# Attention in a hybrid decoder step: two heads' scores as row tiles, weighted sums as alternating column tiles, the sample's weighted sum in four column tiles

## The reference, cut to what matters

```python
s = jnp.einsum('bnqrhd,bnkrhd->bnrhqk', qb, kc) + bias      # scores, ALiBi bias
p = jnp.exp(s - lse[..., None])                             # three window patterns
o = jnp.einsum('bnrhqk,bnkrhd->bnqrhd', p, vc)              # weighted sum of the values
...
kg = k_ext[:, idx]; vg = v_ext[:, idx]                      # sample rows: gathered cache rows
s = jnp.einsum('bshd,bsjhd->bshj', q, kg) - slopes * offs
o = jnp.einsum('bshj,bsjhd->bshd', p, vg)
...
o_att = jnp.sum(mix_w[..., None] * o_stack, axis=0).reshape(B, T, D_ATT) * jax.nn.silu(g_a)
```

## Time and profile before

| | |
|---|---|
| median of the runs | 1742.71 us |
| span of the profiled execution | 1741.7 us (the runs' time lies 1.0 us above it; the page gives the execution no time of its own beside the span) |
| PE busy | 1626.1 us, 93% |
| DVE, ACT, POOL busy | 814.8, 571.7, 529.7 us |
| projection matmuls, L442, three forms | 595.6, 531.6, 531.5 us |
| phase B, 8 pairs | seven pairs of 72.00 us from one `ssum` to the next, then 75.07 us |

### The profile page before, as it was taken

The page is one execution under the profiler, slowest core; times in us unless marked ns, Lnnn a source line. Parts: engine busy times, 40 slices in busy tenths (PEclk is TensorE's granted clock), DMA queues, the critical chain, the costliest instruction groups (busy, mean ns, idle before and its releaser), DMA issues.

```text
span 1741.7 us, 32851 instructions
## 1 busy us (share of the span) xinstructions
PE 1626.1 (93%) x12525; PEld 1491.2 (86%) x12525; DVE 814.8 (47%) x1326; ACT 571.7 (33%) x935; POOL 529.7 (30%) x256
## 2 busy tenths in 40 slices
PE   5999989999899998999989999999999999789998
PEld 4988979889798897988979988898888988569998
DVE  3145564655646557465575544263443634420000
ACT  5242232422324223232242333334343343432221
POOL 0333232232322323223142223232232332433432
PEclk9999999999999999999999999999999999899999
DMA  5320220302203022030220544435344363525443
GB/s 185 93 73 18 63 58 3 105 13 62 58 1 103 17 63 58 1 96 25 56 73 26 131 104 121 88 99 139 78 121 98 89 139 78 153 73 146 127 113 87
DMA packets 249819, 140.88 MB, mean 81 GB/s; under 512 B 11053, under 2 KB 242798, under 8 KB 249198
## 3 DMA queue, kind: packets, MB, share of 16 engines
q1 hardware_dynamic: 228156, 126.23, 28.2%
q10 hardware_dynamic: 21570, 13.23, 2.5%
HBM read 124.11 MB, written 15.26 MB: 80 GB/s over the span
## 4 chain that ended last, share of the span: by engine, by line
PE 84%; DVE 7%; issue 4%; ACT 1%; DMA 1%; SPq 1%; POOL 1%; DVEq 0%; ACTq 0%; POOLq 0%
PE acc L442 50%; PE head_banks L858 5%; PE head_banks L882 5%; PE head_banks L1035 2%; PE head_banks L1062 2%; PE head_banks L1017 2%; PE head_banks L894 2%; DVE AREN L1523 2%; PE head_banks L1029 1%; DVE AREN L1585 1%; PE head_banks L792 1%; PE head_banks L759 1%; DVE AREN L1763 1%; PE head_banks L775 1%; PE head_banks L910 1%
## 5 line engine op out<-in xcount | busy, mean ns | idle before, releaser
L426 POOL TENSOR_TENSOR WL<-WR,WH 128x1024 fp32r<-128x1024 f32 (+1 forms) x164 | 397.8, 2426 | 943.4 <-ACT WH L418 935.2
L442 PE MATMUL acc<-XH,WH 128*128 128x260 f32 (+1 forms) x2624 | 595.6, 308 | 20.1 <-POOL XL L692 10.3
L442 PE MATMUL acc<-XL,WH 128*128 128x260 f32 (+1 forms) x2624 | 531.6, 284 | 0.0
L442 PE MATMUL acc<-XH,WL 128*128 128x260 f32 (+1 forms) x2624 | 531.5, 284 | 0.0
L442 PEld LDWEIGHTS acc<-XH,WH 128*128 128x128 f32 (+1 forms) x2624 | 412.0, 191 | 59.6 <-issue 29.3
L442 PEld LDWEIGHTS acc<-XL,WH 128*128 128x128 f32 (+1 forms) x2624 | 408.2, 190 | 0.0
L442 PEld LDWEIGHTS acc<-XH,WL 128*128 128x128 f32 (+1 forms) x2624 | 407.5, 190 | 0.0
L418 ACT ACTIVATE WH<-WR 128x1024 fp32r<-128x1024 f32 (+1 forms) x164 | 171.7, 1047 | 147.0 <-PE acc L442 123.9
L652 POOL TENSOR_TENSOR AREN<-AREN,CA 128x1024 f32<-128x1024 f32 x40 | 87.0, 2176 | 163.6 <-PE head_banks L858 81.3
L1226 ACT ACTIVATE AREN<-head_banks 128x512 f32<-128x512 f32 x80 | 47.9, 599 | 215.2 <-PE head_banks L894 114.1
L858 PE MATMUL head_banks<-AREN 128*128 128x128 f32 x640 | 89.4, 299 | 22.0 <-DVE AREN L1585 19.3
(11 more groups left out here) (234 smaller groups left out, 1939.1 us busy)
## 6 DMA issues: line engine op xcount, KB each, us to landing
WR<-in_w_in SPq DMA_DIRECT2D x128, 512.0 KB, 4.1
WR<-in_w_out SPq DMA_DIRECT2D x32, 512.0 KB, 5.8
out<-AREN ACTq DMA_DIRECT2D x32, 256.0 KB, 2.7
AREN<-in_cache_k_win SPq DMA_DIRECT2D x16, 384.0 KB, 8.5
AREN<-in_cache_v_win SPq DMA_DIRECT2D x16, 384.0 KB, 8.6
mix_scratch<-AREN ACTq DMA_DIRECT2D x16, 260.0 KB, 2.6
AREN<-in_x_prompt SPq DMA_DIRECT2D x4, 1024.0 KB, 7.9
AREN<-in_cache_k_win SPq DMA_DIRECT2D x8, 512.0 KB, 7.3
```

The costliest lines, as they stand in the source:

```text
L426: pool.tensor_tensor(WL[:, k % 2, :, 0:M], WR[:, k % 4, :, 0:M], WH[:, k % 2, :, 0:M].bitcast(F32), ALU.subtract).then_inc(s_lo, 1)
L442: mm = pe.matmul(acc[0:M, hf, 0:HT], w[:, k % 2, j, 0:M], x[:, kt, hf * HT:(hf + 1) * HT], start=(kt == 0 and n == 0), stop=(kt == KT - 1 ...
```

## The change

- The order of the steps becomes block by block: (b, h) = (0,0), (0,1), (1,0), (1,1) and so on.
- `QP` with its zero halves becomes `QN`. The scores of the two heads are two matmuls with 64 rows each, on partitions 0 to 63 and 64 to 127, into banks 0 and 1, issued one behind the other. They wait for the largest value (`mx`) of the second head of the block before.
- The weighted sums of both heads are issued together after the second head's transposes, alternating between output partitions 0 to 63 and 64 to 127. They are written to the same 128 columns of bank 3 for every block, so DVE multiplies by the gate block by block (`mixed`, step mo{b}), and the second head's transposes go to bank 3 also and wait for mo{b-1}.
- `av` has twelve matmuls of 256 columns instead of six of 512: the weights have 32 columns (16 used, 16 zero), and the four groups of output columns go to partitions 0, 32, 64 and 96 of one bank. ACT copies once, and `avt` is two transposes of 128 by 128. DVE's last product is four operations instead of two.
- `BEHIND_B` has 12 units at `qb` instead of 14, none at the first head's score, 2 at the second's, 2 at every transpose; the rest moves behind `avt`. `BEHIND_LAST` is as before.
- The copy `QS` of the sample queries falls away; one DVE operation forms `QN` instead of two.

```diff
-JS = [(h, b) for h in range(2) for b in range(QB)]
-BEHIND_B = {"ssum": 6, "tokv": 2, "stok": 2, "qb": 14,
-            **{f"s{j}": (1, 1, 2, 2)[j % QB] for j in range(len(JS))},
-            **{f"t{j}": (1, 2, 2, 2)[j % QB] for j in range(len(JS))},
+JS = [(h, b) for b in range(QB) for h in range(2)]
+BEHIND_B = {"ssum": 6, "tokv": 2, "stok": 2, "qb": 12,
+            **{f"s{j}": 2 if j % 2 else 0 for j in range(len(JS))},
+            **{f"t{j}": 2 for j in range(len(JS))},
             "sct": 4, "pwt": 3, "av": 2}
+PT_BANK = (2, 3, 2, 3, 2, 3, 2, 1)
...
-                    pe.matmul(HB[:, j % 2, 0:n], QP[:, h, 128 * b:128 * (b + 1)], KN[:, 0:n], start=True, stop=True)\
-                        .then_inc(b_pe, PE_B.one(f"s{j}"))
-                    fill(f"s{j}")
+                    pe.wait_ge(b_dve, DVE_B.at(i, f"mx{2 * b - 1}" if b else "pr2"))
+                    for h in range(2):
+                        rows = slice(HD * h, HD * (h + 1))
+                        pe.matmul(HB[:, h, 0:n], QN[rows, 128 * b:128 * (b + 1)], KN[rows, 0:n], start=True, stop=True)\
+                            .then_inc(b_pe, PE_B.one(f"s{2 * b + h}"))
+                    fill(f"s{2 * b + 1}")
...
+                for b in range(QB):
+                    if b + 1 < QB:
+                        score(b + 1)
+                    for h in range(2):
+                        j = 2 * b + h
+                        pe.wait_ge(b_dve, DVE_B.at(i, f"pn{j}"))
+                        pe.wait_ge(b_act, ACT_B.at(i, f"tp{j - 1}" if j else "stok"))
+                        if h and b:
+                            pe.wait_ge(b_dve, DVE_B.at(i, f"mo{b - 1}"))
+                        for t in range(b + 1):
+                            mm = pe.transpose(HB[:, PT_BANK[j], 128 * t:128 * (t + 1)], PP[:, h, 128 * t:128 * (t + 1)], ident)
+                        mm.then_inc(b_pe, PE_B.one(f"t{j}"))
+                        fill(f"t{j}")
+                    pe.wait_ge(b_act, ACT_B.at(i, f"tp{2 * b + 1}"))
                     for t in range(b + 1):
+                        for h in range(2):
+                            cols = slice(HD * h, HD * (h + 1))
+                            mm = pe.matmul(HB[cols, 3, 384:512], VTOK[:, t, cols], PTR[:, h, 128 * t:128 * (t + 1)],
+                                           start=(t == 0), stop=(t == b), skip_group_check=True)
...
-                for q in range(2):
-                    for t, n in enumerate(TS):
-                        mm = pe.matmul(HB[0:16, 2 * q, :], PW[0:n, t, :],
-                                       VC[0:n, t, 4 * q:4 * q + 4, :].rearrange("p b c -> p (b c)"),
-                                       start=(t == 0), stop=(t == 2))
+                for t, n in enumerate(TS):
+                    for q in range(4):
+                        mm = pe.matmul(HB[32 * q:32 * (q + 1), 2, 0:256], PW[0:n, t, :],
+                                       VC[0:n, t, 2 * q:2 * q + 2, :].rearrange("p b c -> p (b c)"),
+                                       start=(t == 0), stop=(t == 2), skip_group_check=True)
...
-                for b in range(NB):
-                    mm = pe.transpose(HB[:, 1, 16 * b:16 * (b + 1)], PRF[0:16, 128 * b:128 * (b + 1)], ident[0:16, 0:16])
+                for e in range(2):
+                    mm = pe.transpose(HB[:, 1, 128 * e:128 * (e + 1)], OS[:, e, :], ident)
...
+                def mixed(b):
+                    dve.wait_ge(b_pe, PE_B.at(i, f"o{b}"))
+                    if b == 0:
+                        dve.wait_ge(o_mix, done(PAIRS, i, 16))
+                    q = slice(128 * b, 128 * (b + 1))
+                    dve.tensor_tensor(MIXB[:, q], HB[:, 3, 384:512], GGB[:, q], ALU.mult).then_inc(b_dve, DVE_B.one(f"mo{b}"))
...
                     if j + 2 < nj:
                         largest(j + 2)
+                    if j and h == 0:
+                        mixed(b - 1)
```

More of the change, by code:

```diff
@@ L1361, in pair_b @@
                     feed(f"s{j}")
+                for j in range(2):
                     exps(j)
@@ L1364, in pair_b @@
                     n = 128 * (b + 1)
-                    if j + 2 < nj:
+                    if h == 0 and j + 2 < nj:
                         feed(f"s{j + 2}")
+                        feed(f"s{j + 3}")
                     act.wait_ge(b_pe, PE_B.at(i, f"t{j}"))
-                    act.activation(PTR[:, j % 2, 0:n], HB[:, 2, 0:n], ACT.Copy).then_inc(b_act, ACT_B.one(f"tp{j}"))
+                    act.activation(PTR[:, j % 2, 0:n], HB[:, PT_BANK[j], 0:n], ACT.Copy).then_inc(b_act, ACT_B.one(f"tp{j}"))
                     if j + 2 < nj:
@@ L1391, in pair_b @@
                 act.wait_ge(b_pe, PE_B.at(i, "av"))
-                for q in range(2):
-                    avc = act.activation(PRF[0:16, 512 * q:512 * (q + 1)], HB[0:16, 2 * q, :], ACT.Copy)
-                avc.then_inc(b_act, ACT_B.one("avc"))
+                act.activation(OS.rearrange("p e c -> p (e c)"), HB[:, 2, 0:256], ACT.Copy).then_inc(b_act, ACT_B.one("avc"))
                 feed("av")
@@ L1703, in pair_b @@
                                          op0=ALU.mult, op1=ALU.mult).then_inc(b_dve, DVE_B.one("kn"))
-                for h in range(2):
-                    rows = slice(HD * h, HD * (h + 1))
-                    qn = dve.scalar_tensor_tensor(out=QP[rows, h, :], in0=ZB[rows, 0, :], scalar=QW[rows, 0:1],
-                                                  in1=RNB[rows, 0, :], op0=ALU.mult, op1=ALU.mult)
-                qn.then_inc(b_dve, DVE_B.one("qn"))
-                after("qn")
-                for h in range(2):
-                    rows = slice(HD * h, HD * (h + 1))
-                    qs = dve.tensor_copy(QS[rows, :], QP[rows, h, T:TT])
-                qs.then_inc(b_dve, DVE_B.one("qs"))
+                dve.scalar_tensor_tensor(out=QN, in0=ZB[:, 0, :], scalar=QW[:, 0:1], in1=RNB[:, 0, :],
+                                         op0=ALU.mult, op1=ALU.mult).then_inc(b_dve, DVE_B.one("qn"))
                 dve.wait_ge(s_cb, 16)
@@ L1789, in pair_b @@
                     rows = slice(HD * h, HD * (h + 1))
-                    ms = dve.tensor_tensor(MIXB[rows, T:TT], HB[rows, 1, h:128:18],
-                                           GGB[rows, T:TT], ALU.mult)
+                    for e in range(2):
+                        at = 130 * e + h
+                        ms = dve.tensor_tensor(MIXB[rows, T + e:TT:2], HB[rows, 1, at:at + 109:36],
+                                               GGB[rows, T + e:TT:2], ALU.mult)
                 ms.then_inc(b_dve, DVE_B.one("mixs"))
```

61 lines of the change are left out of this document (20 added, 41 removed).

## The result

The changed kernel took 1693.14 us (median of 4 runs, 1691.56 to 1693.83), the kernel before 1743.12 us beside it (with a fourth run beside the three named above, 1742.65 to 1746.49). The ratio is 0.9704, with a 95% interval of 0.9692 to 0.9716: 50.0 us less, where 57.9 less were predicted. That lies inside the range (1668 to 1703), and 0.1 us outside the likeliest case's own range (1677 to 1693).

The account below looks back on a forecast made before the run. PE's time plus few waits was taken as the bound. Per pair, -9.10 us of PE time and +1.3 of waits made -7.8; seven pairs -53.9, the last -4.0: 1742.7 - 57.9 = 1684.8 us, range 1668 to 1703 (likeliest case 1677 to 1693).

Parts of the forecast that it names:

- terms 4 and 5: PE time per pair: `av` as four column tiles side by side gains 3.82 us; `avt` as two full transposes gains 0.57.
- Terms 1 and 2: PE time per pair: both heads' scores side by side gain 2.15 us; their weighted sums side by side gain 2.20.
- Term 3: PE time per pair: visits to tile modes fall from 2.72 to 2.36 us, a gain of 0.36.
- passage from column to row tiles: PE going from weighted sums straight to scores: taken as 0.20 us, with bounds 0 and 0.40.
- rivals A and E: Four `av` tiles overlapping by two or none, 1695 or 1715, chance 0.14; all tiles serial, loads exposed, 1813, chance 0.02.
- Rival D: Column tiles in weighted sums and `av`: weight loads are exposed, 36 us more, 1721 us; chance 0.03.
- t0's wait: PE's wait at t0 for pn0, which met POOL's operation, goes: 0.7 us less per pair, bounds 0 and 0.7.
- The two new ones: New PE waits where DVE meets POOL: 0.3 us at t1 and 1.7 at t7 per pair, each with bounds 0 and 2.4.
- Rival C: New waits at t1 and t7 don't come, and the passage between tile kinds may be free: 1667 to 1671; chance 0.09.
- Rival B: The vector chain replaces PE as the limit, t1 and t7 at their upper bounds: 19.6 us more, 1704; chance 0.10.
- Pair 0: First pair of heads in phase B: no wait at t0 to lose, so 0.7 us less gain than the usual 7.8.
- The last pair: Eighth pair: scores and sums gain nothing; `av` and `avt` gain 4.4 us, less 0.4 for later tiles, so -4.0.

Follow-up runs that it names:

- e5: The changed kernel with `av` undone: six matmuls of 512 columns, two ACT copies and eight small transposes, as before the change; 1727.49 us.
- e3: The changed kernel with 11 instead of 12 projection units behind `qb`, the unit taken away moved to the pair's end; 1674.61 us.
- e6: The kernel before, in its old order, with each head's scores multiplying only its own 64 rows, one score at a time; 1763.46 us.
- e2: The changed kernel with 10 instead of 12 projection units behind `qb`, the two taken away moved to the pair's end; 1678.97 us.
- e7: The changed kernel with each score reading all 128 rows against zero-padded queries, one score after the other; 1697.24 us.
- e4: The changed kernel with the same matmuls grouped by tile instead of alternating, in the weighted sums and `av`; 1709.24 us.
- e1: The changed kernel with DVE's product mo2 moved behind pn7, PE waiting for it ahead of o3 instead of t7; 1685.1 us.

## Why the prediction was right, and where it was off

**What bounds it.** Right: in e5 PE gets 4.39 us of work back with the waits unchanged, and the pair grows by 4.39. The rest of the story is waits.

**The terms of PE time.** Right for four of the five. `av` adds 1.44 (1.29 + 0.10 + 0.05 had been added up), its way out 0.19, `avt` 0.22; e5 measures terms 4 and 5 together at 4.39, the predicted 4.39. Terms 1 and 2 came as said to 0.05. Without its two gaps the pair is 65.08 - 2.65 = 62.43 us of PE, which is what e3 has. Before it was 72.00 less the wait at t0, 0.88 by starts: 71.12. That makes -8.7, where -9.10 was predicted.

**Term 3, the mode changes,** was mis-sized: 0.36 was said, and the chains give about 2.5 before and 2.4 after, a gain of about 0.1. Before, 2.72 had been added up with 0.20 for each way out; but behind a sum with transposes next the way out is 0.15 (o5, o6), and behind o7, ahead of the sample's transposes, 0.11 (0.38 us for 321 columns, which make 0.27 at 0.11 for 128). For the new order 2.36 was added up, and 2.4 came, by luck. Only o0 and o1 are followed by scores, since block b+1's scores are issued ahead of block b's transposes; so what stands above, that a sum is followed at once by a pair of scores once for each block, holds for two of the four, and the sum of the prediction took three. The second pair of scores stands between projection work, a visit of its own at 0.40 (the chain has 0.68 there and 1.63 behind it). That is 0.20 more than was counted, and the ways out behind o2 and o3, 0.15 + 0.11 instead of 0.40, are 0.14 less.

**The passage from column to row tiles**, taken as 0.20 between 0 and 0.40: the scores behind a sum add 0.84 (384 columns) and 1.06 (512), 0.20 over 0.64 and 0.85. The choice held, and e6 has it again (1.05).

**Four tiles in one round.** The rivals A and E are out: 24 passes of 256 columns, at half of 0.43 each 5.2 us one after the other, take 1.44 with entry and first load. The first passes of the four tiles start within 0.02 us, and the later rounds follow 0.22 us apart, the time of one pass: four-fold. The Trainium skill (TensorE: Matmul & The Clock Gate, Part 3, measured speedup) has 2.38 for three column tiles; by that share `av` would have been about 1.7 us, an estimate. The trace disagrees, for four tiles with six passes each. Rival D, and the rule behind it, are out too: o3 puts sixteen passes and 0.14 of entry in 1.02 us, which is eight rounds of 0.11, so no load shows. Its numbers were too low besides: 0.106 is the distance between the loads of the earlier trace rows, whose single records last 0.137 us, and the ten pairs of matmuls are twenty rounds of passes, not ten.

**The waits.** This is the other step that was off, in size and not in kind. That t0's wait goes was right (0.7 in the list, 0.88 by starts). The two new ones stood at the places named, by the mechanism named: at t1 0.79 instead of 0.3, at t7 1.86 instead of 1.7. For t7, POOL starts 0.1 us ahead of the end of o2 (1159.60 against 1158.88 + 0.83), not 0.1 behind, and pm7 ends 0.55 us behind POOL. For t1 the sum was made to "POOL's end, 0.3 after PE wants t1"; POOL's end came about when PE wants t1, but behind it, at 1143.34, stand the end of pm1, a reciprocal, pn1 and two signals, 0.80 us until t1 starts. Together +1.77 net instead of +1.3. So a pair lost 6.92 where 7.8 was said; of the 0.88 between them 0.47 is waits, and 0.41 the terms of PE time, of which some 0.25 is term 3. Rival C (no new waits, 1671, or 1667 with a free passage) is nearly what e3 reached by one number, 1674.61. Rival B, DVE as the limit, happened at neither t1 nor t7; but in e2 the first scores wait 0.5 us for DVE's products for the sample, so that is what comes next.

**Pair 0** lost 6.84 where 7.1 was said. **The last pair** lost 6.36, not 4.0. Scores and sums there gained nothing, as said (28.7 us from the first score to `sct`, 28.3 before); `av` and what follows it gained 5.24, where 4.4 less 0.4 was said; and the stretch ahead of the scores, which the change doesn't touch, ran 1.5 us shorter. There 24 projection matmuls add 4.74 us at a granted clock of 0.62, 5.57 before at 0.50; and behind `avt` 54 of them add 8.28 at 0.79, 9.09 before at 0.71. So the 2.4 us by which the last pair beat its forecast are mostly the clock, and luck. Why the clock did so isn't settled.

**What the prediction had no term for.** Phase A and phase C together took 5.1 us more in the profiled run, on unchanged code. Phase A ended at 978.7 us before and at 981.3 after, and at 978.1 to 981.2 in six experiments, which have the same phase A too (983.6 in e7, where a buffer is cleared besides). Phase C took 178.4 us before and in e5, 179.9 in e7, and 180.8 to 181.0 in the changed kernel and the others, e6 among them, which has the old order. It is its first six projection units that differ: 36 matmuls right behind a wait of PE for ACT and POOL, which is about 4.3 us long in both kernels.

```profile
1514.64 7.15 PE acc L445 x36
```

7.15 us at a granted clock of 0.60, against 4.61 at 1.00 before for the same 36; at the full level, 2.4 GHz, the same 36 take 4.31 in a pair, so most of the 7.15 ran at 1.2 GHz. Why isn't settled.

Added up by spans, 8.2 us lie between prediction (-57.9) and result (-49.7): 5.3 are the 0.88 of each of six pairs, 0.3 pair 0, 5.1 the two phases, and the last pair's 2.4 go the other way. So two differences that nobody forecast partly cancel. The two phases and the last pair are read from single profiles, and how much of them is in the medians isn't shown; the runs of the kernel before, without any change, spread from 1741.51 to 1748.31 us over the experiments.

## What to carry to other kernels

In this kernel tiles of TensorE paid only beside a partner, and the passes of different tiles had to alternate in the program as soon as a tile had more than four in a row: grouped by tile, four column tiles took 2.81 us instead of 1.44, and row tiles without a partner made a pair 1.71 us slower. When PE's program gets shorter, look at where GpSimd's long operations between SBUF buffers now fall against the vector operations that PE waits for, and move one number of the fill table before making the chain itself shorter: here that was worth 18.5 us, over a third of what the rewrite had brought. Put both ends of a collision in the sum: the wait ends not with GpSimd's operation, but after all that stands behind it on DVE. And count the visits to a tile mode from the program's order, with what really follows each.

## What the runs showed of the hardware

- PE starts a pass of another tile ahead of its turn when it stands at most four passes behind one that is starting: the second tile's first pass starts 0.005 us behind the fifth of the first in o3, and 0.005 and 0.006 us behind the third in o2 and `av` (e4). Up to four passes of one tile in a row cost nothing (0.37 and 0.60 us, as alternating).
- Four column tiles of 32 columns run fully side by side: 24 passes in 1.44 us, entry included; the same columns one after the other take 5.26 (e5).
- The way out of column tiles depends on what follows: 0.19 or 0.20 us before projection work or scores, 0.15 before t6 and t7, and 0.11 before the sample's transposes with their 16 weight columns (behind o7 before the change, o3 after it).
- Which DVE operations wait for POOL's L429, and which don't. L1761 (two SBUF inputs) took 2.52 instead of 0.29 and 2.59 instead of 0.69, and the tensor-scalar L1769 with one SBUF input 2.59 instead of 0.49. But L1751, with one input in PSUM, took 0.29 beside it, as always, and so did these two, of which one has an input in PSUM and the other is a reduction of one SBUF buffer (the second runs into POOL's last 0.7 us):

```profile
1135.04 2.40 POOL L429 TENSOR_TENSOR WL<-WR,WH 128x1024 fp32r<-128x1024 f32 x1 [5.17 <-ACT WH L421]
1135.48 1.22 DVE L1723 TENSOR_TENSOR AREN<-AREN,head_banks 96x1024 f32<-96x1024 f32 x1
...
1136.73 1.22 DVE L1727 TENSOR_REDUCE AREN<-AREN 96x16 f32<-96x1024 f32 x1
```

  The Trainium skill (SBUF — State Buffer, the section on SBUF's two separate sides) says that a vector operation with two SBUF inputs, or in a mode that uses both ports, and a GpSimd operation that reads SBUF, as L429 does, exclude each other for a whole instruction. The rows agree that the later one is held up, down to the 0.08 us by which pn7 came too late in e1. Whether L1769 runs in a mode with both ports no row says. And not all of the later one's time comes behind POOL's end: the three operations end 0.14, 0.55 and 0.28 us behind it, 0.14 to 0.21 us less than each takes alone. The other way round, in e1 L1769 started 0.06 us ahead of POOL (1146.88) and kept its 0.42 us, while POOL's operation took 2.57 instead of 2.39.
